# Expert weights read by rows that lie together, with the contraction order of the expert products changed to match

## The reference

```
hid = silu(t @ w_gate[e]) * (t @ w_up[e])
out = out + combine[:, e:e + 1] * (hid @ w_down[e])
```

## Time and profile before

| | us |
|---|---|
| median of 3 runs | 2575.82 |
| lowest and highest | 2569.62, 2578.47 |
| span of the profiled execution | 2571.9 |
| PE busy in the span | 2185.8 |
| PEld busy in the span | 1278.1 |
| DVE busy, ACT busy | 708.8, 392.8 |
| share of the span of the DMA queue of SP, on 16 engines | 76.2% |
| moved from HBM | 727.29 MB, 284 GB/s |

### The profile page before, as it was taken

One profiled execution on the slowest core, in us unless ns is written; L12 is line 12 of the kernel. 1 busy time (PEld: TensorE's weight loads), 2 busy tenths in 40 slices (PEclk: granted clock), 3 DMA queues, 4 the chain that ended last, 5 costly groups with the idle time before them and its releaser, 6 DMA issues. The chain is left out here.

```text
span 2571.9 us, 31833 instructions
## 1 busy us (share of the span) xinstructions
PE 2185.8 (85%) x12595; PEld 1278.1 (50%) x12595; DVE 708.8 (28%) x1605; ACT 392.8 (15%) x729; POOL 0.3 (0%) x5
## 2 busy tenths in 40 slices
PE   1475579999999795799999998995966799999997
PEld 0354345555555343455555554553753355555554
DVE  3367431111111346221111112003463221111112
ACT  0002211111111103111111111002320111111111
POOL 0000000000000000000000000000000000000000
PEclk9986679999999898889999999997567799999999
DMA  7575289999999582779999995442003789999994
GB/s 200 163 268 201 80 313 350 400 404 402 400 404 400 207 286 87 280 284 402 400 404 401 400 405 199 150 146 51 1 0 132 279 308 401 400 405 400 401 404 171
DMA packets 331448, 732.31 MB, mean 285 GB/s; under 512 B 18832, under 2 KB 44771, under 8 KB 331259
## 3 DMA queue, kind: packets, MB, share of 16 engines
q1 hardware_dynamic: 331388, 731.52, 76.2%
HBM read 727.29 MB, written 4.21 MB: 284 GB/s over the span
## 5 line engine op out<-in xcount | busy, mean ns | idle before, releaser
L231 PE MATMUL psum<-arena 128*64 128x256 f32 x6144 | 682.0, 379 | 2.5 <-ACT arena L320 2.5
L231 PEld LDWEIGHTS psum<-arena 128*64 128x64 f32 x6144 | 436.4, 136 | 245.1 <-issue 36.8
L900 PE MATMUL psum<-arena,hT 128*128 128x512 f32 (+2 forms) x1088 | 415.2, 544 | 21.9 <-DVEq L920 14.9
L245 PE MATMUL psum<-arena 128*64 128x512 f32 x1536 | 350.9, 598 | 0.0
L900 PEld LDWEIGHTS psum<-arena,hT 128*128 128x128 f32 x1088 | 211.5, 195 | 222.6 <-issue 199.8
L215 PE MATMUL psum<-arena,h 128*128 128x128 f32 x1632 | 215.4, 287 | 26.0 <-ACT arena L332 22.0
L215 PEld LDWEIGHTS psum<-arena,h 128*128 128x128 f32 x1632 | 196.6, 197 | 56.3 <-ACT arena L332 33.4
L438 DVE TENSOR_TENSOR arena<-arena,psum 128x256 f32<-128x256 f32 x96 | 40.6, 423 | 599.7 <-ACT arena L328 599.7
L245 PEld LDWEIGHTS psum<-arena 128*64 128x64 f32 x1536 | 101.4, 136 | 207.0 <-issue 201.2
L221 PE MATMUL psum<-arena 128*128 128x512 f32 x408 | 196.9, 605 | 3.0 <-DVE arena L305 3.0
L305 DVE COPY arena<-psum 64x512 f32<-64x512 f32 x96 | 66.8, 695 | 364.4 <-PE psum L245 364.4
(11 more groups left out here) (242 smaller groups left out, 1187.1 us busy)
## 6 DMA issues: line engine op xcount, KB each, us to landing
arena<-in_moe_w_dram SPq DMA_DIRECT2D x192, 2048.0 KB, 18.3
arena<-in_w_gate_dram SPq DMA_DIRECT2D x32, 2048.0 KB, 18.1
arena<-in_w_up_dram SPq DMA_DIRECT2D x32, 2048.0 KB
arena<-in_w_down_dram SPq DMA_DIRECT2D x32, 2048.0 KB, 18.7
arena<-in_ada_w_dram SPq DMA_DIRECT2D x24, 2048.0 KB
arena<-in_w_in_dram SPq DMA_DIRECT2D x12, 1800.0 KB, 6.9
arena<-in_odd_w_in_dram SPq DMA_DIRECT2D x6, 2048.0 KB, 7.8
arena<-in_even_w_in_dram SPq DMA_DIRECT2D x8, 1160.0 KB
```

Source lines behind the costliest of these rows:

```text
L231: m = nc.tensor.matmul(out[64 * half:64 * half + 64, :], xg[:, c, BLOCK * u:BLOCK * (u + 1)], w[:, c, half * HALF:(half + 1) * HALF], star ...
L245: m = nc.tensor.matmul(bank_Y[64 * half:64 * half + 64, :], hTs[:, k % 2, (k // 2) * 64:(k // 2) * 64 + 64], experts.slots[slot][2][:, k, ...
L900: m = nc.tensor.matmul(banks[2 * u + t][:, 0:width], inT[:, k, t * P:(t + 1) * P], wt[:, u, k, :], start=(k == 0), stop=(k == kc - 1))
```

## The change

The rows of the weight matrices are dealt to the partitions in another order. For w1 and w3, partition `p` now holds rows `8p` to `8p + 7`, which are 16 KB that lie together in HBM. For w2, each half of the 512 rows is dealt on its own: partition `p` holds rows `2p` and `2p + 1` of each half, so two pieces of 8 KB. Each matrix is still one DMA of 2 MB into the same place.

A contraction is a sum over rows, so its other operand has to be dealt in the same way. Piece `cc` of the gather therefore takes the features `cc`, `cc + 8`, `cc + 16` ...: its stationary operand is read with a step of 8 elements (32 bytes) where it was contiguous. Piece `c` of the transposed hidden layer takes the hidden columns `c`, `c + 2`, ...: a step of 2 elements (8 bytes). The number, kind and order of instructions on every engine are as before, and so are their semaphores; where a row of the program has a number over 85, it has one more in the changed kernel.

```
-        pairs = lambda w: w.rearrange("(j two) (c p) n -> two j p c n", two=2, p=P)
-        self.w1, self.w3, self.w2 = pairs(w1), pairs(w3), pairs(w2)
+        ups = lambda w: w.rearrange("(j two) (p c) n -> two j p c n", two=2, p=P)
+        self.w1, self.w3 = ups(w1), ups(w3)
+        self.w2 = w2.rearrange("(j two) (half p c) n -> two j p half c n", two=2, half=2, p=P)
...
-        sp.dma_start(self.slots[slot][2], self.w2[u, pair]).then_inc(self.w2_landed[slot], 16)
+        sp.dma_start(self.slots[slot][2].rearrange("p (half c) n -> p half c n", half=2), self.w2[u, pair]).then_inc(self.w2_landed[slot], 16)
...
-                        m = nc.tensor.matmul(XG[:, c, :], h[:, t, cc * P:(cc + 1) * P], sel[:, t, :],
+                        m = nc.tensor.matmul(XG[:, c, :], h[:, t, cc::DC], sel[:, t, :],
                                              start=(t == 0), stop=(t == 1))
...
-                    m = nc.tensor.transpose(HT[:, c, :], hm[:, c * P:(c + 1) * P], ident[:, :])
+                    m = nc.tensor.transpose(HT[:, c, :], hm[:, c::2], ident[:, :])
```

## The result

| | before | changed |
|---|---|---|
| median of the runs | 2575.09 (4) | 2775.81 (4) |
| lowest and highest | 2569.62, 2578.47 | 2771.22, 2780.23 |
| span of the profiled execution | 2571.9 | 2778.5 |
| PE busy, PEld busy | 2185.8, 1278.1 | 2391.3, 1483.4 |

The changed kernel is slower by 7.9%: the ratio is 1.0786, with a 95% interval from 1.0761 to 1.081. Between the medians lie 200.7 us. The numbers in parentheses are the runs shown.

What follows compares the result with a forecast made beforehand. TensorE was taken to bound the kernel. To the profiled 2571.9 us came 164 for the gather's strided loads, 0 for the transposes and 0 for the DMAs: 2736, stated as 2740 us against the runs' median, range 2568 to 2775.

Steps and rivals of the forecast that it cites:

- What bounds the kernel: In the expert stages TensorE sets the pace, 30.08 us a pair of experts; faster weight loads are worth 0.
- Where the price falls: In the gather's stationary loads, which follow without a gap, so nearly all of any slowdown appears in the pair's time.
- the term for the price of a load: Gather loads at a 32-byte step: +107 ns each, from a VectorE row giving 62 to 154; 1536 records, +164 us.
- likeliest case: Gather slower by the strided loads: 2671 to 2812 us, with 2740 taken; chance 0.52.
- The spare 9 ns: Slack of each gather load between two gather matmuls; would take 14 us from the loss, but was left out.
- The first gathers: 96 gather records before the stages' first pairs, at the lower clock: taken as 0, with 10 us kept for the range.
- The transposes: 192 stationary loads at a step of 8 bytes: taken as 0 because the step is small, 21 us kept for the range.
- The loads: Weight DMAs behind a slower gather: no more lead lost, SP waiting longer late in a stage, traffic falling to 376 GB/s.
- No change: Rival: the step costs TensorE nothing, 2576 us; holds if the mean of the gather's loads stays below about 200 ns; chance 0.33.
- Far slower: Rival: each gather column needs VectorE's full 1.65 ns twice over, +484 us, 3060 us; chance 0.05.
- late weights: Rival: larger pieces load slower and reach TensorE late, below about 391 GB/s; 2620 us at 380 GB/s; chance 0.04.
- Something is won: Rival: longer pieces free a barrier or a stage's first loads, less than 10 us, 2566 us; chance 0.06.

Runs made afterwards that it cites:

- The transfers alone: The changed kernel with the gather's and transposes' operands read contiguously again, so only the weights' layout differs from the kernel before: 2569.77 us, ratio 0.9986.
- the light kernel: Long pieces, contiguous operands, gather of one token tile and half the scatter, against the kernel before: 2442.48 us, ratio 0.9485; with short pieces 2520.68 us.

## Why the prediction was right, and where it wasn't

I had forecast 2740 us, within a range of 2568 to 2775, and 2775.81 were measured. The direction and the mechanism were right; one term of the sum was too small.

- **What bounds the kernel: right.** TensorE sets the pace, and faster loads are worth nothing. The transfers alone show it: 419 for 401 GB/s, and no measurable gain.
- **Where the price falls: right.** Loads without a gap show their price in full. 3.88 us for 1.86 in the loads of each of two parts became 4.03 us more in the pair.
- **The step that failed: the term for the price of a load, which was mis-sized.** I took +107 ns, the middle of a bracket of 62 to 154. One part's 16 loads measure (3.88 - 1.86) / 16 = **+126 ns**. 1536 x 0.126 = 194 us, where I had 164. The bracket, with its likeliest case of 2671 to 2812 us, held the result; the range that I gave did not. I cut its top at 2775 to reach down to the case of no change, and the result is 0.8 us above. A bracket worked out from another engine's row has no preferred middle, and its upper half should not have been what I gave away. The row was also at another step, and that is the missing part: at VectorE's 64 bytes TensorE pays 0.221 - 0.116 = 0.105 us, and 0.126 only at 32 bytes. That the middle of the bracket meets the first of these is luck.
- **The spare 9 ns: not there.** 4.03 us over the 32 records of a pair are 126 ns each, all of what the loads became longer. I had left it out of the sum.
- **The first gathers: wrong.** I took 0 for the 96 records, with the reason that they run at the lower clock and a column there already has 1.66 ns. They cost 5.3 us in all, inside the 10 that I kept. At the lower clock a record pays 0.244 - 0.219 = 0.025 us, a fifth of the price at the full clock, so the reason was nearly right. But 4 to 16 of the 32 records before had already run at the full clock, and these pay in full.
- **The transposes: right number, wrong reason.** 0 us on the path, with loads that did get longer (197 ns for 140). The check that I named, about 250 ns, was too far off to catch this.
- **The loads: right, with sizes off.** They no longer lose lead, SP's waits stay long late in a stage, and no wait of TensorE in an expert stage ends with a DMA. Traffic fell to 369 to 372 GB/s; I had 376 for the shorter pair that I forecast.
- **The rivals.** "No change" fell by its own test (L216's loads at 334 ns, bound 200). "Far slower" and "late weights" fell; the point that I gave for late weights behind a slower gather, 365 GB/s, should have been about 354, since the 16 us of lead that are no longer used count too (29 us over 29 experts, 6.29 MB in 17.75 us). "Something is won" fell for the changed kernel. The transfers alone leave it open within their interval, but not at the first barrier: from the first prefetch to the issue behind the barrier SP takes 25.56 us with them (329.19 to 354.75) and 25.54 before (325.46 to 351.00).
- **The rule of the Trainium skill** that I set beside the row held in both parts, one hit to a line slow and two nearly free (step 2: 0.128 us for 0.120).

## What to carry to other kernels

An order of rows in memory is also an order of columns in the other operand: count what the engine that reads it loses before what the transfer gains. For float32 on TensorE at the full clock, a step of 2 elements costs 6% of a load of 128 columns and a step of 4 or 8 doubles it; the moving operand pays the same at step 8. It is free where the load has idle time before it and falls in full on the path where loads follow each other. Take the price from a row at the same step: 64 bytes cost less than 32. Longer pieces raised the rate of the loads from 401 to 429 GB/s, which matters only if they set the pace, so find out first whether a DMA ever ends a wait.

## What I had not expected of the hardware

- **VectorE was a good ruler for the whole time of a strided element, and a poor one for the surcharge.** At a step of 64 bytes VectorE takes 1.65 ns an element and TensorE's load 0.221 / 128 = 1.73 ns a column. At 32 bytes VectorE's add in the norm stage that writes in the dealt order takes (1.08 - 0.158) / 512 = 1.80 ns, and TensorE's load 0.243 / 128 = 1.90. Contiguous they differ, 1.04 and 0.91, and so do the surcharges. Both engines are slower at 32 bytes than at 64, and TensorE's time does not go with its clock. This speaks for one limit outside the engines; no run shows what it is.

```profile
359.35 1.14 DVE L765 SCALAR_TENSOR_TENSOR h<-x,norm_sums,norm_w 128x512 f32<-128x512 f32 x1
360.52 1.08 DVE L767 TENSOR_TENSOR h<-h,arena 128x512 f32<-128x512 f32 x1
```

- **The issue of a DMA on SP takes long when earlier loads are still under way.** The number of its own pieces does not decide alone. The same load of w3 with 1024 pieces of 2 KB took SP 0.37 us to issue early in the first stage of the kernel before, and 8.25 later, when the loads had lost their lead:

```profile
394.68 0.37 SPq L93 DMA_DIRECT2D arena<-in_moe_w_dram  x1
...
651.14 8.25 SPq L93 DMA_DIRECT2D arena<-in_moe_w_dram  x1
```

  Short pieces bring this about sooner: of the six loads issued in a row before the first barrier, the longest issue took 7.79 us with the short pieces and 1.09 with the long ones. With 128 pieces of 16 KB it took 0.33 us in the changed kernel, where the loads are always ahead, and 5.45 in the light kernel, where they are late:

```profile
1307.13 0.33 SPq L94 DMA_DIRECT2D arena<-in_moe_w_dram  x1
```

```profile
734.99 5.45 SPq L94 DMA_DIRECT2D arena<-in_moe_w_dram  x1
```

- **The limit of the traffic moves with the pieces:** 401 GB/s with 2 and 4 KB, 429 with 16 and 8, both where TensorE waits for the weights. The runs that TensorE paces had 419 (16 and 8 KB) and 416 (4 and 8 KB); these are no limits.
